# Two pools of weight buffers, cut another way: five raw and five rounded slots in place of seven and four, and ten pieces for tile 0 first at stage ends

## The reference

```
def first_block(x, ...):
    h = rms_norm(x, mix_norm_g[l])
    proj = h @ w_in[l]
    q, kv, gate_logits, conv_in = jnp.split(proj, splits, axis=-1)
    attn = nsa_attention(q, kv, gates, rel_bias, cmp_pos[l], cmp_w1[l], cmp_w2[l])
    conv = conformer_conv(conv_in, conv_w[l], conv_b[l], conv_ln_g[l], conv_ln_b[l])
    x = x + jnp.concatenate([attn, conv], axis=-1) @ w_out[l]
    h = rms_norm(x, ffn_norm_g[l])
    x = x + conv_glu_ffn(h, w_up[l], ffn_conv_w[l], ffn_conv_b[l], w_down[l])
    return rms_norm(x, final_norm_g)

def second_block(x, c, ...):
    ada = jax.nn.silu(c) @ w_ada[l] + b_ada[l]
    shift_m, scale_m, gate_m, shift_f, scale_f, gate_f = ...split of ada...
    h = rms_norm_2(x, g_pre_mix[l]) * (1.0 + scale_m) + shift_m
    ...latent attention and gated linear attention of h @ w_in[l]...
    x = x + gate_m * rms_norm_2(o, g_post_mix[l])
    h = rms_norm_2(x, g_pre_ffn[l]) * (1.0 + scale_f) + shift_f
    f = (jax.nn.silu(h @ w_ffn_gate[l]) * (h @ w_ffn_up[l])) @ w_ffn_down[l]
    x = x + gate_f * rms_norm_2(f, g_post_ffn[l])
```

## Time and profile before

| | |
|---|---|
| Time, median of 3 runs | 2238.95 us (2235.58, 2238.95, 2239.26) |
| Profiled execution | 2235.5 us, of which the span is 2233.7 us |
| PE busy | 2193.6 us (98%) |
| DVE busy | 1611.1 us (72%) |
| ACT busy | 1119.3 us (50%) |
| DMA, mean over the span | 226 GB/s |

### The profile page before, as it was taken

The page is one execution under the profiler, slowest core; times in us unless marked ns, Lnnn a source line. Parts: engine busy times, 40 slices in busy tenths (PEclk is TensorE's granted clock), DMA queues, the critical chain, the costliest instruction groups (busy, mean ns, idle before and its releaser), DMA issues.

```text
span 2233.7 us, 30478 instructions
## 1 busy us (share of the span) xinstructions
PE 2193.6 (98%) x12130; PEld 1883.6 (84%) x12130; DVE 1611.1 (72%) x2423; ACT 1119.3 (50%) x1670; POOL 29.6 (1%) x63
## 2 busy tenths in 40 slices
PE   7999999999999999999989999989999999999998
PEld 7999887888888888888879787878888888888986
DVE  6998885899998799998865655566555555544555
ACT  5434774555554455554454655555444444444343
POOL 1000000000000000000000000000000000000000
PEclk9999999999999999999999999999999999999999
DMA  8644436688889888889955551647666677655563
GB/s 271 217 162 142 153 97 209 221 294 285 291 301 369 320 281 289 291 287 361 341 157 185 179 179 57 225 134 250 226 228 224 227 230 232 217 188 190 187 211 120
DMA packets 138223, 504.13 MB, mean 226 GB/s; under 512 B 15616, under 2 KB 15760, under 8 KB 137184
## 3 DMA queue, kind: packets, MB, share of 16 engines
q1 hardware_dynamic: 136512, 494.42, 65.5%
q0 software_dynamic: 1280, 5.65, 1.0%
q10 hardware_dynamic: 288, 2.10, 0.3%
HBM read 499.61 MB, written 2.51 MB: 225 GB/s over the span
## 4 chain that ended last, share of the span: by engine, by line
PE 85%; DVE 11%; ACT 2%; issue 1%; DMA 0%; POOL 0%; SPq 0%; DVEq 0%; ACTq 0%; POOLq 0%
PE bank L603 20%; PE both L603 18%; PE bank L606 10%; PE both L606 9%; PE bank L593 7%; DVE w_lo L1623 5%; PE bank L594 4%; PE bank L596 4%; PE bank L598 4%; PE bank L597 4%; DVE raw L1605 2%; ACT ffn_a L1345 1%; ACT ffn_g L1351 1%; PE bank L830 1%; PE both L787 1%
## 5 line engine op out<-in xcount | busy, mean ns | idle before, releaser
L1623 DVE TENSOR_TENSOR w_lo<-raw,w_hi 128x1024 fp32r<-128x1024 f32 x737 | 893.8, 1221 | 450.1 <-ACT w_hi L1147 448.6
L1147 ACT ACTIVATE w_hi<-raw 128x1024 fp32r<-128x1024 f32 x737 | 767.9, 1054 | 640.9 <-PE bank L606 296.6
L593 PE MATMUL bank<-h_both,w_hi 128*128 128x512 f32 x1408 | 356.5, 394 | 1.8 <-DVE h_both L1677 1.8
L593 PEld LDWEIGHTS bank<-h_both,w_hi 128*128 128x128 f32 x1408 | 253.2, 189 | 47.0 <-DVE h_both L1677 2.5
L1605 DVE SCALAR_TENSOR_TENSOR raw<-raw,silu_c 128x1024 f32<-128x1024 f32 x192 | 233.9, 1218 | 0.0
L603 PE MATMUL bank<-w_hi,h_both 128*128 128x512 f32 (+2 forms) x1024 | 233.9, 372 | 0.0
L603 PE MATMUL both<-w_hi,h_both 128*128 128x512 f32 (+1 forms) x960 | 231.9, 383 | 1.7 <-DVE h_both L1697 1.7
L603 PEld LDWEIGHTS bank<-w_hi,h_both 128*128 128x128 f32 x1024 | 181.8, 188 | 33.1 <-issue 0.3
L594 PEld LDWEIGHTS bank<-h_both,w_lo 128*128 128x128 f32 x1408 | 192.1, 190 | 13.7
L603 PEld LDWEIGHTS both<-w_hi,h_both 128*128 128x128 f32 x960 | 171.3, 191 | 34.5 <-DVE h_both L1697 2.9
L594 PE MATMUL bank<-h_both,w_lo 128*128 128x256 f32 x1408 | 196.3, 282 | 0.0
(11 more groups left out here) (366 smaller groups left out, 2624.4 us busy)
## 6 DMA issues: line engine op xcount, KB each, us to landing
raw<-weights SPq DMA_DIRECT2D x924, 512.0 KB, 4.5
raw<-weights SPq DMA_DIRECT2D x5, 504.0 KB, 4.2
x<-x SPq DMA_DIRECT2D x2, 1024.0 KB, 5.6
bias<-bias_rows POOLq DMA_DIRECT2D x8, 256.0 KB, 11.6
silu_c<-c ACTq DMA_DIRECT2D x2, 1024.0 KB, 4.6
gate_row<-gate_rows POOLq DMA_DIRECT2D x2, 1024.0 KB, 8.7
out<-x SPq DMA_DIRECT2D x8, 256.0 KB, 2.1
final_row<-final_row POOLq DMA_DIRECT2D x1, 1024.0 KB, 5.1
```

The costliest lines, as they stand in the source:

```text
L593: return e.matmul(out, hi, a_both[:, k, :, :].rearrange("p a t -> p (a t)"), start=first, stop=last)
L1147: e.activation(w_hi[:, n % PART_SLOTS, 0:widths[i]], raw[:, i % RAW_SLOTS, 0:widths[i]], ACT.Copy).then_inc(hi_ready, 1)
L1623: e.tensor_tensor(w_lo[:, slot, 0:widths[i]], raw[:, i % RAW_SLOTS, 0:widths[i]], w_hi[:, slot, 0:widths[i]].bitcast(F32), ALU.subtract).t ...
```

## The change

The raw slots go from seven to five and the slots of `w_hi` and of `w_lo` from four to five each, so that the memory of the three buffers together stays the same (15 slots). `AHEAD` goes from 3 to 4 with it. `TILEWISE` becomes ten pieces, five chunks, at the ends of `down1` and `down2`, and nine pieces at that of `out2`; the end of `out_attn` keeps eight, and the place at which ACT stops before loading `c` stays where it was.

```diff
--- before.py
+++ after.py
@@ -44,8 +44,8 @@
 
 
 CHUNK = 1024
-RAW_SLOTS = 7
-PART_SLOTS = 4
+RAW_SLOTS = 5
+PART_SLOTS = 5
 AHEAD = PART_SLOTS - 1
 
 
@@ -378,7 +378,7 @@
         f2_parts, f2_total, f2_factor = stats(TT * 4), stats(TT), stats(TT)
         FINAL_ORDER = ["x0", "x1", "g0", "g1", "x2", "g2", "x3", "g3"]
         SQUARES_OUT1, SQUARES_FINAL, SQUARES_O2, SQUARES_F2 = 2, 10, 26, 42
-        TILEWISE = 8
+        TILEWISE = 2 * PART_SLOTS
         NU = TT * HEADS
         cmp_max, cmp_sum, cmp_coef = stats(NU), stats(NU), stats(NU)
         neg_max, row_sum, coef = stats(2 * NU), stats(2 * NU), stats(2 * NU)
@@ -875,7 +875,7 @@
             tiles["of"], tiles["turn"] = (4, 5, 2, 3), 0
             for n in range(4):
                 pair = (2 * (n % 2), 2 * (n % 2) + 1)
-                group(("out_attn", n), 512, pair, mix_hi, mix_lo, attn_need, TILEWISE if n == 3 else 0)
+                group(("out_attn", n), 512, pair, mix_hi, mix_lo, attn_need, KD // 2 if n == 3 else 0)
                 free[pair[0]], free[pair[1]] = (residual, 8 + 2 * n + 1), (residual, 8 + 2 * n + 2)
 
             need = h_need(1, lambda k: (h_ready, 16 + k + 1))
@@ -1307,7 +1307,7 @@
             for n in range(4):
                 if n == 0:
                     load_c()
-                    round_until(groups["out_attn", 0][TILEWISE // 2 - 1][0])
+                    round_until(groups["out_attn", 0][KD // 4 - 1][0])
                     silu_of_c(0)
                 round_until(lead(final["out_attn", n]) if n < 3 else final["out_attn", n])
                 for tt in range(TT):
```

## The result

| | before | changed |
|---|---|---|
| median, 20 runs each | 2235.57 us (2234.82 to 2239.26) | 2241.26 us (2237.65 to 2245.29) |
| profiled execution, span | 2235.5, 2233.7 us | 2240.4, 2238.6 us |
| granted clock, mean | 0.994 | 0.994 |

The ratio is 1.0023, 95% interval 1.0016 to 1.0029: 5 us slower (3.6 to 6.5; the two medians lie 5.7 us apart), just beyond the 0.2% that the prediction called no change. The kernel before, whose first three runs had a median of 2238.95, is at 2235.57 over twenty.

A forecast was written before the change was run, and what follows sets the result against it. TensorE was taken as the bound, busy 2193.6 of 2233.7 us. The terms 0 - 0.6 + 0.1 + 0 + 0.35 + 0.3 = +0.15 us, on a median of 2238.95, gave 2239.1 us; range 2234.5 to 2246.5.

The forecast's parts named there:

- no change: Whole kernel: each stretch keeps its cushion and small terms cancel, within 0.2% (4.5 us), 2236.5 to 2242; chance 0.64.
- the rival that five raw slots starve `down1`: In `down1` loads fall below the 339 GB/s asked for: +3 us a half, 2242 to 2245; chance 0.24.
- Part 1: Stage ends: ten pieces for tile 0 first start its norm 1.36 us earlier, but tile 1 ends the wait: 0.
- Part 2: TensorE's wait at 654 us goes with more rounded slots, -0.6 us; the next chunk comes late, +0.1.
- Part 3: Under the convolution taps, 163 to 191 us, DVE sets the 3.11 us period; more slots give 0.
- Part 4: `cmp_w1` holds four of five raw slots; DVE waits 2.6 us and the rest TensorE needs comes later: +0.35 us.
- Part 5: Five raw slots where `up` and `down1` use the DMA hard: pace just kept, cushion used up, +0.3 us.

The follow-up runs named there:

- `cmp_w1` edit: Changed kernel with ScalarE's and VectorE's look-ahead behind `cmp_w1` cut from three chunks to one: median 2241.28 us, ratio 1.0022.
- short look-ahead: Kernel before with a look-ahead of one chunk behind `cmp_w1` in place of three: median 2235.93 us, ratio 1.0000.

## Why the prediction was right in its range and wrong in its centre

I forecast no change with 0.64 and +0.15 us; it is +5 us, in the range, by the rival that five raw slots starve `down1` (0.24). This rival had a hold of 2.8 us and +3 us for one starved half, close to what came. That the time lies even in the narrower range given for no change, 2236.5 to 2242, is luck: it was laid around 2238.95, the median of three runs, and twenty put the kernel before 3.4 us lower.

- **Part 1, the tile pass: right, 0.** The last wait ends with tile 1; undoing the pass changes nothing.
- **Part 2, the wait at 654: mechanism right, size wrong.** The wait of 0.62 us is gone (the matmuls there are 0.8 us earlier), but these two came in its place:

```profile
657.74 0.70 PE L603 MATMUL both<-w_hi,ff_hi 128*128 128x512 f32 x2 [0.43 <-ACT w_hi L1147]
...
669.28 0.70 PE L603 MATMUL both<-w_hi,ff_hi 128*128 128x512 f32 x2 [0.24 <-ACT w_hi L1147]
```

  With smaller ones beside them TensorE loses 1.3 us. The first 0.7 of it belongs here, where I had put +0.1 and bounded it at 1.5: in sum -0.1 in place of -0.5. The other 0.7, up to 670, stands behind waits of ScalarE for landings (5.01 us before 664.87, 2.15 before 668.08) and belongs to part 5.
- **Part 3, the taps: right.** In the changed kernel the period is still 3.11 us, so a fifth rounded slot cured nothing. The Trainium skill (Perfetto Trace Analysis, Optimization Strategy) says that a repeating gap can mean a lack of buffers; this one didn't:

```profile
178.13 1.20 DVE L1623 TENSOR_TENSOR w_lo<-raw,w_hi 128x1024 fp32r<-128x1024 f32 x1
...
181.24 1.21 DVE L1623 TENSOR_TENSOR w_lo<-raw,w_hi 128x1024 fp32r<-128x1024 f32 x1
```

  What shortened it, in the profiles of two kernels, was order: fewer taps left to do in the stretch. Their medians didn't show the gain.
- **Part 4, `cmp_w1`: right.** 2.74 us of idle time on DVE for 2.6, and +0.45 us for +0.35.
- **Part 5, the term that failed: "I take +0.3 for both halves".** The rate was right at 672 to 728 (348 GB/s forecast, 348 measured), and there the pace was kept. The hold of a slot was not right: 1.8 us forecast, 2.4 there, and 2.8 in the second half. I had counted only the instructions that work on the chunk. A chunk is also held while ScalarE and VectorE do something else, and an ada chunk until DVE has come to it, behind rests that wait for ScalarE. With 2.8 us and a landing of 5.3 the slot goes round in 8.1 us, more than the 7.7 that 339 GB/s allow, so the lead isn't rebuilt in the second half; the sum of the prediction had the margin the other way. And I had looked for what the lead must cover only at the start of the stage. Here it has to cover the ends of column blocks with their squares, the longest of them ScalarE's block of six (4.9 us), before which the lead was 7 us in the trace before and 0.6 in the changed one. Measured are +3.5 us for this half, 0.5 above its bound of +3, and +0.7 for the other, in place of +0.3 for both.

That raw slots and landings cause the loss is shown from three sides: the slots alone (2241.0), one slot more (2235.7), and fewer bytes in the second half of `down1` with the same slots (2236.7, with an interval apart from that of the changed kernel), which also says where nearly all of it is lost. That slots are held too long at the ends of column blocks is read from the traces; no run moved the squares at 1050 and 1080 or the work at 1097 away. That the block of six turns lateness into one large stall is seen in the trace of the changed kernel, but taking it apart changed no median by itself (2240.9), and with the `cmp_w1` edit (2238.6) the profile puts the gain elsewhere.

## What to carry to other kernels

With a ring of buffers in a stretch where the loads barely keep pace, compute the time of one round, landing plus hold, and take the hold from the trace, from landing to the next issue into that slot, not from the durations of the instructions. Look at the hold where the engines do other work, not only where they follow each other smoothly: here it was 2.3 us for most split chunks and up to 5.5 at the ends of column blocks. Then compare the lead with the longest block of other work where it stands, not on average. And before a profile is used to rank two versions, see where its execution lies among the runs: between traces of nearly the same kernel the loss in one stage was 1 to 5 us. Two pools with the same total are not the same: here the seventh raw slot was free to give away, the sixth was not.

## What the runs showed of the hardware beyond that

- Loads of 512 KB land in 4.7 us in the median with four slots, 5.2 with five, 5.5 with six and 5.7 with seven (5.5 in a second trace with seven), all issued from 672 to 728: the landing shrinks with fewer under way, but more slowly than the slots are taken away.
- TensorE's clock falls for short stretches at the same places in some executions and not in others. The granted clock from 200 to 204 us was 0.65 in the kernel before with the short look-ahead and 0.67 with eight pieces, so for part of the time at the lower of its levels, 1.2 GHz, and 1.00, 2.4 GHz, in the traces of the kernel before and of the changed one. TensorE was busy without a gap from 196 in all four. Such a stretch costs 1.5 us there. With gains of 1 to 2 us one profile can thus mislead in either direction.
